# Attention in a two-layer transformer kernel: items taken by pairs, scores in turns on TensorE's two row halves, V products in turns on its two column halves

## What is computed

```python
# layer 0: 8 heads of sparse attention (own keys by a top-64 choice) and 8 heads of block attention
s = einsum('bqhd,bkhd->bhqk', q, k) * 64 ** -0.5     # head dimension 64, causal mask
p = masked_softmax(s, mask)
o = einsum('bhqk,bkhd->bqhd', p, v)
# layer 1: 16 heads in 4 groups; three attentions over compressed, selected and window keys
o = gc[..., 0:1] * o_c + gc[..., 1:2] * o_s + gc[..., 2:3] * o_w
# both layers: cross attention to the memory, 4 heads of dimension 128
s = einsum('bshd,bmhd->bhsm', q, k) * 128 ** -0.5
o = einsum('bhsm,bmhd->bshd', softmax(s), v)
```

## Time and profile before

| | |
|---|---|
| median of 3 runs | 1623.06 us (1621.54 to 1623.09) |
| the profiled execution, its time | 1621.49 us |
| its span, first to last instruction | 1619.5 us |
| PE busy, share of the span | 1451.1 us, 90% |
| PE's weight loads | 1190.7 us, 74% |
| DVE busy | 1093.2 us, 68% |
| ACT busy | 735.8 us, 45% |
| POOL busy | 88.1 us, 5% |
| mean granted clock of PE | 0.922 of full |

### The profile page before, as it was taken

One profiled execution on the slowest core, in us unless ns is written; L12 is line 12 of the kernel. 1 busy time (PEld: TensorE's weight loads), 2 busy tenths in 40 slices (PEclk: granted clock), 3 DMA queues, 4 the chain that ended last, 5 costly groups with the idle time before them and its releaser, 6 DMA issues.

```text
span 1619.5 us, 18427 instructions
## 1 busy us (share of the span) xinstructions
PE 1451.1 (90%) x6769; PEld 1190.7 (74%) x6769; DVE 1093.2 (68%) x1805; ACT 735.8 (45%) x897; POOL 88.1 (5%) x177
## 2 busy tenths in 40 slices
PE   6877996899998878996899998997969999999996
PEld 5655675788886776785788876785768888888884
DVE  4787456655555855666655557777549797979795
ACT  4343334444334302434444443364337676767673
POOL 0000211000000002411000000050000000000000
PEclk9989587999999966998999999998969999999997
DMA  6442004355555410013356654443727797979890
GB/s 227 157 143 104 14 27 143 111 185 188 190 182 156 128 46 1 1 45 125 130 185 192 192 175 139 169 136 113 291 79 294 274 369 273 362 278 356 286 355 36
DMA packets 123509, 277.62 MB, mean 171 GB/s; under 512 B 15382, under 2 KB 68780, under 8 KB 108076
## 3 DMA queue, kind: packets, MB, share of 16 engines
q1 hardware_dynamic: 121168, 275.99, 49.7%
q10 hardware_dynamic: 2268, 0.65, 0.2%
HBM read 275.57 MB, written 1.05 MB: 171 GB/s over the span
## 4 chain that ended last, share of the span: by engine, by line
PE 73%; DVE 14%; ACT 6%; issue 4%; DMA 2%; ACTq 1%; POOL 0%; DVEq 0%; SPq 0%
PE bank L1877 19%; PE bank L1879 18%; PE bank L1878 18%; PE bank L1965 4%; PE bank L1983 3%; DVE t_wlo L1128 3%; PE bank L2254 2%; PE bank L1972 2%; DVE t_wlo L1139 2%; DMA t_raw<-in_ab_w_in 1%; ACT t_whi L750 1%; PE bank L1951 1%; PE bank L2110 1%; ACT t_whi L737 1%; ACT t_z L775 1%
## 5 line engine op out<-in xcount | busy, mean ns | idle before, releaser
L1128 DVE TENSOR_TENSOR t_wlo<-t_raw,t_whi 128x2048 fp32r<-128x2048 f32 (+3 forms) x144 | 316.3, 2206 | 145.4 <-ACT t_whi L737 143.0
L1877 PE MATMUL bank<-t_whi,t_ahi 128*128 128x512 f32 (+3 forms) x832 | 331.5, 398 | 34.6 <-DVE t_wlo L1128 15.4
L737 ACT ACTIVATE t_whi<-t_raw 128x2048 fp32r<-128x2048 f32 (+3 forms) x144 | 263.8, 1840 | 165.8 <-PE bank L1879 142.6
L1877 PE MATMUL bank<-t_whi,t_bhi 128*128 128x512 f32 (+1 forms) x800 | 314.7, 393 | 24.4 <-DVE t_z L1765 6.5
L1879 PE MATMUL bank<-t_whi,t_alo 128*128 128x512 f32 (+3 forms) x832 | 325.9, 392 | 0.0
L1878 PE MATMUL bank<-t_wlo,t_ahi 128*128 128x512 f32 (+3 forms) x832 | 325.7, 391 | 0.0
L1879 PE MATMUL bank<-t_whi,t_blo 128*128 128x512 f32 (+1 forms) x800 | 308.6, 386 | 0.0
L1878 PE MATMUL bank<-t_wlo,t_bhi 128*128 128x512 f32 (+1 forms) x800 | 308.5, 386 | 0.0
L1877 PEld LDWEIGHTS bank<-t_whi,t_ahi 128*128 128x128 f32 x832 | 160.2, 193 | 73.4 <-issue 29.6
L1877 PEld LDWEIGHTS bank<-t_whi,t_bhi 128*128 128x128 f32 x800 | 153.4, 192 | 56.3 <-issue 19.0
L1879 PEld LDWEIGHTS bank<-t_whi,t_alo 128*128 128x128 f32 x832 | 159.5, 192 | 32.3
(11 more groups left out here) (347 smaller groups left out, 1532.3 us busy)
## 6 DMA issues: line engine op xcount, KB each, us to landing
t_raw<-in_ffn_w_in SPq DMA_DIRECT2D x88, 512.0 KB, 4.7
t_raw<-in_ffn_w_out SPq DMA_DIRECT2D x22, 1024.0 KB, 4.9
t_raw<-in_w_in SPq DMA_DIRECT2D x18, 1024.0 KB, 5.1
t_raw<-in_exp_w_up SPq DMA_DIRECT2D x18, 1024.0 KB, 6.8
t_raw<-in_exp_w_down SPq DMA_DIRECT2D x18, 1024.0 KB, 6.6
t_raw<-in_exp_w_gate SPq DMA_DIRECT2D x15, 1024.0 KB, 6.7
t_memo<-in_exp_w_gate SPq DMA_DIRECT2D x13, 1024.0 KB, 6.9
t_feat<-in_exp_w_up SPq DMA_DIRECT2D x13, 1024.0 KB, 7.3
```

The lines of the kernel that those rows point to most:

```text
L737: act.activation(whi[slot][:, 0:n], raw[slot][:, 0:n], ACT.Copy).then_inc(hi_done, 1)
L1128: dve.tensor_tensor(wlo[slot][:, 0:n], raw[slot][:, 0:n], whi[slot][:, 0:n].bitcast(F32), ALU.subtract).then_inc(lo_done, 1)
L1877: pe.matmul(dst, lhi, rhi_, start=start, stop=False)
```

## The change

Items are taken by pairs `(t, t + 1)`, and the loops step by two.

- **PE, scores**: both items' scores in one go, in turns: branch 0 of the first, branch 0 of the second, branch 1 of the first, branch 1 of the second. The two items of a pair lie in different row halves and write to different banks. In layer 1 the list of items is put in another order for that: heads are paired so that the row half and the output half of the two both differ, and both items have the same chunk, so the same number of keys.
- **PE, V products**: of the pair in round `t - 6`, again in turns, so that the output halves (columns 0 to 63 and 64 to 127) take turns. They now wait for both copies of the pair. For the memory (`abreast=False`) the V products are issued one item after the other, since an item takes all columns.
- **Copies**: the first item's transposed probabilities are copied by DVE, the second's by ACT. ACT therefore gets a copy (L821 of the changed kernel) in each round, and PE waits for both engines' semaphores.
- **DVE's round** begins with the reciprocals of the pair before, then the masks of this pair, then the copy of item `t - 4`.
- **Banks**: in layer 1 the heads' outputs are placed otherwise (`head_out1`, `bank_chunks`), so that a bank's two column blocks hold heads four apart.

The diff, cut to its core:

```diff
 
-        run = Run(n, per, self.item(n), self.outs, self.turn(n, 0, 1), self.emptied, tiles)
+        batch = self.turns
+        for _ in range(n // 2):
+            self.turn(1, 0, 1)
+            self.turn(1, 1, 0)
+        run = Run(n, per, self.item(n), self.outs, batch, self.emptied, tiles)
         self.outs += n
...
+        def head_out1(k, half_, c):
+
+            return G[2 * (k // 4) + k % 2][DH * half_:DH * half_ + DH, T * (k // 2 % 2) + P * c:T * (k // 2 % 2) + P * c + P]
+
+        def bank_chunks(k, apart):
+
+            return slice(4 * (k // 2) + k % 2, 4 * (k // 2) + k % 2 + 3, 2) if apart else slice(2 * k, 2 * k + 2)
...
-            for h in list(range(8, 16)) + list(range(8)):
-                (jq, half_), g = place1(h), h // 4
-                r = slice(DH * half_, DH * half_ + DH)
-                for c in range(C):
+            for h0 in (8, 10, 0, 2):
+                for h, c in [(h0 + i + (4 + (i ^ 1) - i if second else 0), c) for i in range(2) for c in range(C) for second in range(2)]:
+                    (jq, half_), g = place1(h), h // 4
+                    r = slice(DH * half_, DH * half_ + DH)
                     nk, q = P * (c + 1), 2048 + T * jq + P * c
                     branches = [Branch(feat[r, q:q + P], keys[r, T * (g // 2):T * (g // 2) + nk], nk, causal[:, c, 0:nk],
                                        [Z1[:, b, v0 + DH * g:v0 + DH * g + DH] for b in range(c + 1)],
-                                       head_out(h // 2, h % 2, c))
+                                       head_out1(h // 2, h % 2, c))
                                 for keys, v0 in ((feat[:, 4096:4608], VSEL), (KWT, VWIN))]
                     out_.append(Item(branches, DH ** -0.5, GATE[:, c, 3 * h + 1:3 * h + 3],
                                      (VBLK[:, g, h % 4, :], CPT[c][:, P * g:P * g + P])))
...
+            def attention(items, run, banks, apart=False):
 
                 n, per = run.n, run.per
-                for t in range(n + 5 + 1):
+                for t in range(0, n + 6, 2):
                     if t < n:
-                        it, g = items[t], run.first + t
-                        act.wait_ge(item_masked, g + 1)
-                        if t >= 4:
-                            act.wait_ge(turned, run.batch + t - 3)
-                        for m in range(2):
-                            a_, b_ = it.at[m], it.at[m] + it.branches[m].nk
-                            ins = act.activation(run.prob[g % 4][:, a_:b_], run.masked[g % 2][:, a_:b_], ACT.Exp, scale=-1.0,
-                                                 bias=item_min[:, 2 * t + m:2 * t + m + 1],
-                                                 accum_out=item_sum[:, 2 * t + m:2 * t + m + 1])
-                        ins.then_inc(exped, 1)
-                    if t >= 5 and (t - 4) % per == 0:
+                        for i in (t, t + 1):
+                            it, g = items[i], run.first + i
+                            act.wait_ge(item_masked, g + 1)
+                            if i >= 4:
+                                act.wait_ge(turned, run.batch + i - 3)
+                            for m in range(2):
+                                a_, b_ = it.at[m], it.at[m] + it.branches[m].nk
+                                ins = act.activation(run.prob[g % 4][:, a_:b_], run.masked[g % 2][:, a_:b_], ACT.Exp, scale=-1.0,
+                                                     bias=item_min[:, 2 * i + m:2 * i + m + 1],
+                                                     accum_out=item_sum[:, 2 * i + m:2 * i + m + 1])
+                            ins.then_inc(exped, 1)
+                    if 0 <= t - 4 < n:
+                        i = t - 3
+                        act.wait_ge(turned, run.batch + i + 1)
+                        if i >= 2:
+                            act.wait_ge(pved, run.outs + i - 1)
+                        w = items[i].width
+                        act.activation(run.probt[1][:, 0:w], TB[(run.batch + i) % 2][:, 0:w], ACT.Copy).then_inc(turn_act, 1)
+                    if t >= 6 and (t - 4) % per == 0:
                         k = banks[(t - 4) // per - 1]
                         act.wait_ge(pved, run.outs + t - 4)
-                        act.activation(ahi[:, 2 * k:2 * k + 2, :], G[k][:, :].rearrange("p (k t) -> p k t", k=2),
+                        act.activation(ahi[:, bank_chunks(k, apart), :], G[k][:, :].rearrange("p (k t) -> p k t", k=2),
                                        ACT.Copy).then_inc(heads_hi, 1)
 
...
-            def attention(items, run, banks):
+            def attention(items, run, banks, apart=False):
 
                 n, per = run.n, run.per
-                for t in range(n + 5 + 1):
+                for t in range(0, n + 6, 2):
+                    if 0 <= t - 2 < n:
+                        for i in (t - 2, t - 1):
+                            inv = item_inv[:, 2 * i:2 * i + 2]
+                            dve.wait_ge(exped, run.first + i + 1)
+                            ins = dve.reciprocal(inv, item_sum[:, 2 * i:2 * i + 2])
+                            if items[i].weight is not None:
+                                step(ins)
+                                ins = dve.tensor_tensor(inv, inv, items[i].weight, ALU.mult)
+                            ins.then_inc(item_weighed, 1)
                     if t < n:
-                        it, g = items[t], run.first + t
-                        dve.wait_ge(scored, g + 1)
-                        if t >= 2:
-                            dve.wait_ge(exped, g - 1)
-                        for m, b_ in enumerate(it.branches):
-                            s_ = slice(it.at[m], it.at[m] + b_.nk)
-
-                            ins = dve.tensor_tensor_reduce(run.masked[g % 2][:, s_], SCB[g % 2][:, s_], b_.bias, -it.scale,
-                        i = t - 3
+                        for i in (t, t + 1):
+                            it, g = items[i], run.first + i
+                            dve.wait_ge(scored, g + 1)
+                            if i >= 2:
+                                dve.wait_ge(exped, g - 1)
+                            for m, b_ in enumerate(it.branches):
+                                s_ = slice(it.at[m], it.at[m] + b_.nk)
+
+                                ins = dve.tensor_tensor_reduce(run.masked[g % 2][:, s_], SCB[g % 2][:, s_], b_.bias, -it.scale,
+                                                               -TAKEN, ALU.add, ALU.min, item_min[:, 2 * i + m:2 * i + m + 1])
+                            ins.then_inc(item_masked, 1)
+                    if 0 <= t - 4 < n:
+                        i = t - 4
                         dve.wait_ge(turned, run.batch + i + 1)
                         if i >= 2:
                             dve.wait_ge(pved, run.outs + i - 1)
                         w = items[i].width
-                        dve.tensor_copy(run.probt[i % 2][:, 0:w], TB[(run.batch + i) % 2][:, 0:w]).then_inc(turn_dve, 1)
-                    if t >= 5 and (t - 4) % per == 0:
+                        dve.tensor_copy(run.probt[0][:, 0:w], TB[(run.batch + i) % 2][:, 0:w]).then_inc(turn_dve, 1)
+                    if t >= 6 and (t - 4) % per == 0:
                         bank_ = (t - 4) // per
                         k = banks[bank_ - 1]
                         dve.wait_ge(heads_hi, run.banks + bank_)
-                        dve.tensor_tensor(alo[:, 2 * k:2 * k + 2, :], G[k][:, :].rearrange("p (k t) -> p k t", k=2),
-                                          ahi[:, 2 * k:2 * k + 2, :].bitcast(F32), ALU.subtract).then_inc(heads_lo, 1)
+                        dve.tensor_tensor(alo[:, bank_chunks(k, apart), :], G[k][:, :].rearrange("p (k t) -> p k t", k=2),
...
-            def attention(items, run):
+            def attention(items, run, abreast=True):
 
                 n = run.n
-                for t in range(n + 4):
-                        ins.then_inc(turned, 1)
+                        g = run.first + t
+                        if t or run.first >= 2:
+                            pe.wait_ge(item_masked, g)
+                        for m in range(2):
+                            for i in (t, t + 1):
+                                it = items[i]
+                                b_ = it.branches[m]
+                                ins = pe.matmul(SCB[(run.first + i) % 2][:, it.at[m]:it.at[m] + b_.nk], b_.q, b_.k, start=True, stop=True)
+                                if m == 1:
+                                    ins.then_inc(scored, 1)
...
-                        for m, b_ in enumerate(it.branches):
-                            for b, v in enumerate(b_.v):
-                                a_ = it.at[m] + P * b
-                                ins = pe.matmul(b_.out, v, run.probt[i % 2][:, a_:a_ + P], start=b == 0 and not it.first,
+                                ins = pe.transpose(bank[:, P * b:P * b + P], run.prob[(run.first + i) % 4][:, P * b:P * b + P], ident[:, :])
```

(21 more changed lines are left out.)

42 lines of the change are left out of this document (8 added, 34 removed).

## The result

The changed kernel takes **1595.29 us** (median of 4 runs, 1593.71 to 1600.78) against 1622.53 us of the kernel before (4 runs, 1621.54 to 1623.09). The ratio is 0.9837, with a 95% interval of 0.9818 to 0.9856: 27 us faster. The forecast was 1592, its range 1580 to 1612. The profiled execution is the slowest of the four, 1600.78 us with a span of 1599.0, so its own account comes to less than the median's.

What follows compares the result with a forecast made beforehand. PE was taken to bound layers 0 and 1, the chain through the engines the memory. Layer 1 -17, layer 0 -23, memory +7 make -33; hand-overs add 3, so -30 from 1621.5: 1592 us, range 1580 to 1612.

Steps and rivals of the forecast that it cites:

- V products at half: PE, layers 0 and 1: V products in two column halves overlap fully, so a pair costs half; bounds nothing saved or half.
- The rule weighed: PE, V products: weight loads overlap matmuls only where row groups differ, so column halves would wait; prediction counted no weight load.
- rival 2: PE, V products: weight loads hold up the column halves; 1597 with half an overlap, 1603 with none; chance 0.17.
- rival 5: PE, V products: each change of column half empties the array, making the kernel slower, 1638; chance 0.09.
- Rival 4: PE, scores and V products: the tiles don't overlap at all, only switches are saved; 1606; chance 0.08.
- 3.05 + 0.5 a pair: Layer 1 at 2.4 GHz: mean DVE and ACT loop 3.05 us plus bank hand-over 0.5, for 16 pairs, 56.8.
- The ring: DVE and ACT: masks of a pair, both exponentials, second reciprocal, next masks; 2.9 us a pair in layer 0, 3.05 in layer 1.
- the 0.5 a pair for the bank hand-over: Layer 1: ACT and DVE taking a full bank, put at 2.1 us every fourth pair.
- 34.5 forecast: Layer 0 stage: 8 x 3.35 = 26.8, 5.5 at the end, 2 for a slow start, against 57.3 before.
- The early clock: Layer 0: clock rises early because 64-row scores, which kept it low, get shorter; 34.5 us, or 40 if it stays low.
- 3.5 each, bounds 2 to 5: Memory attentions: each longer by one exponential (1.1), half of 2.10 of V products, and 1.3 of scores; +7 together.
- ACT's copy at nothing: ACT's new copy, 0.57 us for 512 columns, costs nothing inside the loops; without cover 0.6 a pair, 14 us.

Runs made afterwards that it cites:

- e5: e1 with both items of a pair in the same row half and output half, so nothing overlaps in layers 0 and 1; 1615.79 us.
- e4: Changed kernel with the memory attentions back in the order of the kernel before, pairs kept in layers 0 and 1; 1587.63 us.
- e8: Changed kernel with both copies of a pair on DVE and ACT's copy removed; 1592.94 us.
- e9: e4 with DVE's round reordered to mask, reciprocal, mask, reciprocal, copy; 1578.0 us.
- e10: e4 with ACT and DVE taking the high and low part of a full bank one round later; 1579.79 us.
- e1: Changed kernel with scores and V products issued item after item instead of in turns, pairs kept; 1595.15 us.
- e7: e1 with layer 1's pairs sharing their output half, so only scores overlap there; 1602.69 us in one execution.

## Why the prediction was right, and where it was off

- **What binds** (PE without gaps in both layers, the chain in the memory): right. PE has gaps now, and the chain left it.
- **Scores of a pair at the price of one item's**: right, 0.70 for two items, by the row it was taken from the earlier trace rows. **V products at half**, for which there was no row: right, 16 records in 1.04, which eight need alone in e5. PE's work of a pair in layer 1 was put at 2.75 us (halving the two terms of its 4.68 gives 2.84); 22.79 of busy time in eight pairs is 2.85.
- **The rule weighed.** No V record waits for the other half's weights: pairs of records start 6 ns apart, all 128 rows in use by both. The Trainium skill's "TensorE: Matmul & The Clock Gate" (Part 3, The mechanism) lets a weight load overlap only where row groups differ; the trace doesn't bear this out for column halves, and rival 2 is out. So is rival 5: the pairs of V records follow each other every 0.109 us with no gap where the half changes. Rival 4 is out by e5, which is the kernel without overlap, at 1615.79.
- **Layer 1**: forecast 3.05 + 0.5 a pair, measured 3.5. The stage is 67.45 rather than 65 because the clock fell again at 667.0, which the forecast had not seen coming: 6 us of PE's work lies in that stretch. e4 and e8, where it did not fall, took 64.1 and 64.4. The split between the terms was less right than their sum. The ring was said to run through DVE and ACT alone, and half of the chain is still PE's own rows. e9's shorter ring takes 0.2 off a round; the rest of e9's gain and all of e10's have no place in the profiles. So the 0.5 a pair for the bank hand-over, which e10 was to take out, is not borne out.
- **Layer 0**: 34.5 forecast (its terms add up to 34.3), 35.35 measured, again with 7.65 us at a fallen clock at its end. e1, e4 and e8, whose clock held, have 33.0, 32.5 and 31.9.
- **The early clock**: right in its size, and in part in its reason. The prediction said that the 64-row scores keep the clock low and that the change shortens just these. In e5 nothing is shortened: 2.92 us for a pair's scores, as before. The clock rose nonetheless, 34 us earlier than before. So about 15 of layer 0's 22 us come with pairing alone. The overlap, with scores in half the time, brought the rise 10 us further ahead (e1 against e5). How much the halved scores would have given by themselves was not tried, and what in the pairs' order lifts the clock is open.
- **Memory, the term that was mis-sized**: "3.5 each, bounds 2 to 5" was 6.2 and 6.9, outside its own bounds. The timeline of memory 0:

```profile
254.79 3.75 PE L1989 MATMUL bank<-t_memo,t_feat 128*128 128x256 f32 x8 [0.83 <-issue]
...
259.42 3.78 PE L1989 MATMUL bank<-t_memo,t_feat 128*128 128x256 f32 x8 [0.87 <-DVE t_item_min L1284]
...
262.38 0.42 DVE L1284 CUSTOM_DVE_ANT_0 t_z<-bank,t_zero 128x256 f32<-128x256 f32 x1 [1.46 <-PE bank L1989]
...
267.44 3.43 PE L2013 MATMUL bank<-t_feat,t_memo 128*128 128x128 f32 x16
269.27 0.69 DVE L1293 COPY t_feat<-bank 128x512 f32<-128x512 f32 x1 [3.21 <-PE bank L2013]
270.97 0.60 ACT L821 ACTIVATE t_feat<-bank 128x512 f32<-128x512 f32 x1 [5.21 <-PE bank L2013]
...
271.62 2.05 PE L2013 MATMUL bank<-t_feat,t_memo 128*128 128x128 f32 x16 [0.75 <-ACT t_feat L821]
```

In the kernel before the third mask was this row of the same view:

```profile
279.05 0.42 DVE L1254 CUSTOM_DVE_ANT_0 t_z<-bank,t_zero 128x256 f32<-128x256 f32 x1 [0.40 <-PE bank L1965]
```

It started 279.05 - 274.00 = 5.05 us into the stage, and now 262.38 - 254.79 = 7.6, 2.5 later: PE waits 0.87 for both masks of the first pair, where its scores ran without a gap before, and then both items' scores stand between. The other 3.8 are in part a wait that I did not follow: the copies of the second pair go into the buffers of the first, so they wait until PE has used them (3.21 and 5.21 us idle). ACT's stands behind the V products of both items, and the last V products behind ACT's. In part they are the clock: the first pair's 16 records take 3.43 us at the low clock, where 2.05 do at the high one, 1.4 more. e1, with the same steps in both memory stages, took 20.2 us at a mean clock of 0.70 and 18.5 at 0.74. Before, each item's products ran beside the next one's copy. I had counted half of the 2.10 of the earlier trace rows, and no wait for a buffer. The sign that I set, 17 to 19 us each, was missed as well.

- **ACT's copy at nothing**: right inside layers 0 and 1 (e8). In the memory ACT's copy is on the chain, as above; e8, with both copies on DVE, still took 19.2 and 20.5 there.
- **The total**: the forecast was -30 from the profiled execution. The profiled execution gave -20.5 of span, the median -27. So the nearness of 1595 to 1592 is in part luck: the stages as profiled missed by 9.5, 6 of them in the memory, and the median execution happened to be faster than the profiled one. Four executions of one kernel lie up to 7 us apart here, where the kernel before has 1.6. The profiles of after and of e9 are each the slowest of their four and each have the clock fallen at the end of layers 0 and 1. In the four of the changed kernel the mean granted clock falls as the time rises: 0.931, 0.929, 0.928 and 0.924 for 1593.71, 1593.89, 1596.68 and 1600.78 us. That the fallen clock makes the spread is likely, not shown, since the three others have no profile.

## What to carry to other kernels

Put neighbours in the instruction stream on different row halves, or different column halves with different banks; that alone runs them side by side. For four records of an item alternation by hand added next to nothing; where an item has eight in a row (V products of 256 keys) it took a pair from 1.53 to 1.04 us, which would count in a kernel that PE still bounds. Then apply the pairing only where tiles leave half of the array free: work that fills it pays for the coarser steps and gets nothing. When PE stops being the bound, look at once at the order in which the other engines take their steps: two small moves there, with the memory taken back, gave 20 us on top of the change's 27, though only a part of that has a place in the profiles.

## What the hardware did that I had not expected

- PE starts a matmul of the other half before earlier ones are begun that the program has ahead: with two items' scores one after the other, both items' first branches start within 13 ns (e1). With eight V records of one item ahead of the other's, the other's first starts 0.44 us late, behind four of them, and the pair takes 1.53 us instead of 1.04.
- Two matmuls that use all 128 rows with different weights run side by side in the two column halves at full rate: 16 records in 1.04 us, against 8 in 1.04 for one half (e7), when the records take turns.
- The clock rose 20 us into layer 0 in e5 with PE busy for 18.23 of 19.70 us and nothing overlapped; the kernel before, with PE busy nearly throughout, held 1.2 GHz for 54 us of the same work in a finer order, and with the overlap it rose after 10 (e1). Coarser order went with an earlier rise, worth about 15 us here; which part of the order does it was not tried.
